# Mixture-of-experts weights fetched with one transfer per matrix instead of four

## The reference, cut to what matters

```python
def ec_moe(x, router_w, w_gate, w_up, w_down):
    bsz, n_tok, _ = x.shape
    cap = n_tok * EC_CAPACITY // N_EXPERTS
    aff = jax.nn.softmax(jnp.einsum('btd,de->bte', x, router_w).astype(jnp.float32), axis=-1)
    gate, idx = lax.top_k(jnp.swapaxes(aff, 1, 2), cap)
    bidx = jnp.arange(bsz)[:, None, None]
    xe = x[bidx, idx]
    hid = jax.nn.silu(jnp.einsum('becd,edf->becf', xe, w_gate)) * jnp.einsum('becd,edf->becf', xe, w_up)
    ye = jnp.einsum('becf,efd->becd', hid, w_down) * gate[..., None].astype(x.dtype)
    return jnp.zeros_like(x).at[bidx, idx].add(ye)
```

## Time and profile before

| | before |
|---|---|
| median of 3 runs | 1393.1 us (1390.18 to 1395.51) |
| the profiled execution, its own time | 1392.07 us |
| its span, first to last instruction | 1390.3 us |
| TensorE busy | 1289.3 us, 93% of the span |
| DVE, ACT, POOL busy | 48%, 35%, 20% |
| bytes moved | 334.27 MB, 240 GB/s on average |
| busy share of the main hardware queue (q1) | 59.0% |
| mean granted TensorE clock | 0.981 |

### The profile page before, as it was taken

How to read it: one execution, slowest core, us unless ns; L and a number is a source line. 1 busy time by engine, 2 the same in 40 slices (tenths; PEclk the granted TensorE clock), 3 DMA queues, 4 the chain that set the end, 5 groups by cost and what they waited for, 6 DMA issues and landing times. The chain is left out here.

```text
span 1390.3 us, 34498 instructions
## 1 busy us (share of the span) xinstructions
PE 1289.3 (93%) x14873; PEld 955.2 (69%) x14873; DVE 665.8 (48%) x1574; ACT 491.9 (35%) x1131; POOL 280.4 (20%) x239
## 2 busy tenths in 40 slices
PE   5999998879899999999989999989999999999996
PEld 1755566756687577777768999555578576777773
DVE  1535614677635243333345646956654433333336
ACT  2723213766423211111125468665533321111113
POOL 0000103596101011111110030645400201111101
PEclk7999999999999999999998999999999999999997
DMA  9688861041448999999982012050065999999985
GB/s 362 233 318 336 334 225 47 5 167 46 157 195 320 365 368 377 375 375 368 369 314 57 1 65 70 1 227 1 1 245 197 391 344 374 376 373 378 376 299 182
DMA packets 105827, 334.27 MB, mean 240 GB/s; under 512 B 23182, under 2 KB 29164, under 8 KB 99532
## 3 DMA queue, kind: packets, MB, share of 16 engines
q1 hardware_dynamic: 99276, 310.11, 59.0%
q0 software_dynamic: 5824, 19.86, 6.1%
q10 hardware_dynamic: 576, 2.10, 0.4%
HBM read 308.13 MB, written 23.89 MB: 239 GB/s over the span
## 5 line engine op out<-in xcount | busy, mean ns | idle before, releaser
L2053 PE MATMUL psum<-proj,wraw 128*64 128x80 f32 x7680 | 285.6, 234 | 14.8 <-issue 14.5
L2053 PEld LDWEIGHTS psum<-proj,wraw 128*64 128x64 f32 x7680 | 272.7, 137 | 32.1 <-issue 29.7
L2102 ACT ACTIVATE proj<-psum,proj 128x64 f32<-128x64 f32 x232 | 67.3, 395 | 289.8 <-PE psum L1981 289.8
L1993 PE MATMUL psum<-wraw,proj 128*32 128x512 f32 x1152 | 156.0, 596 | 2.2 <-ACT proj L2108 1.2
L1959 POOL DMA_INDIRECT x_rows<-modrow,idx x30 | 42.8, 1428 | 430.6 <-DVE modrow L2221 430.6
L2216 DVE SCALAR_TENSOR_TENSOR modrow<-psum,proj 64x512 f32<-64x512 f32 x60 | 44.9, 749 | 132.0 <-PE psum L1999 131.6
L1336 POOL TENSOR_SCALAR ring<-ring,small 128x640 f32<-128x640 f32 x48 | 90.2, 1883 | 40.3 <-DVE small L1275 39.9
L1999 PE MATMUL psum<-wraw,proj 128*16 128x256 f32 x1152 | 96.4, 379 | 1.4 <-issue 0.9
L2176 DVE TENSOR_SCALAR proj<-psum,proj 128x64 f32<-128x64 f32 x232 | 55.7, 317 | 85.4 <-PE psum L1981 85.4
L1999 PEld LDWEIGHTS psum<-wraw,proj 128*16 128x16 f32 x1152 | 35.5, 97 | 80.5 <-issue 73.6
L1266 DVE TENSOR_REDUCE small<-psum 128x1 f32<-128x640 f32 (+1 forms) x80 | 57.3, 716 | 53.8 <-PE psum L1241 53.4
(11 more groups left out here) (524 smaller groups left out, 2366.3 us busy)
## 6 DMA issues: line engine op xcount, KB each, us to landing
wraw<-in_exp_w_gate_dram SPq DMA_DIRECT2D x128, 512.0 KB
wraw<-in_exp_w_up_dram SPq DMA_DIRECT2D x128, 512.0 KB
wraw<-in_exp_w_down_dram SPq DMA_DIRECT2D x128, 512.0 KB
ring<-in_ada_w_dram SPq DMA_DIRECT2D x29, 1024.0 KB, 7.1
hold<-in_ada_w_dram SPq DMA_DIRECT2D x14, 1024.0 KB, 6.7
ring<-in_ev_w_in_dram SPq DMA_DIRECT2D x4, 2048.0 KB, 12.5
xr<-x_rows SPq DMA_DIRECT2D x15, 512.0 KB, 6.6
proj<-in_ada_w_dram SPq DMA_DIRECT2D x5, 1024.0 KB, 8.3
```

Of the source, the lines that this page charges most:

```text
L1993: mm = pe.matmul(psum[quad(q, 32), b, :], xs[:, quad(q % 2, 32)], pair[q // 2], start=first, stop=last)
L2053: mm = pe.matmul(psum[c:c + WT, b, f * CAP:(f + 1) * CAP], wraw[SLOT_OF[m]][:, at:at + WT], rows, start=(k == 0 and f == 0), stop=(k == KD ...
L2102: ins = act.activation(xgT[:, e % 2, k, lo:hi], bank(0)[:, k * CAP + lo:k * CAP + hi], ACT.Identity, scale=scale_of[:, c, k:k + 1], bias=s ...
```

## The change

For all matrices but numbers 4 to 7, `load_weights` issues one transfer of 2 MB where it issued four of 512 KB. In gate and up matrices the row that lands in a partition is now one run of 16 KB. In down matrices it is still four rows of 4 KB. Matrices 4 to 7 still come in four pieces each, as `load_piece` asks for them, and `landed` counts 64 for these and 16 for the others.

```diff
         PARTS = 4
+        IN_PIECES = range(AT_ONCE, AT_ONCE + 4)
...
         def load_weights(sp, l, m, ready):
-            for i in range(PARTS):
-                load_piece(sp, l, m, i, ready)
+
+            n, e = EXPERT_ORDER[m]
+            if n == 2:
+                src, to = A[EXPERT_W[n]][l, e].rearrange("(f p) n -> p f n", p=P), wraw[SLOT_OF[m]][:, :].rearrange("p (f n) -> p f n", f=FB)
+            else:
+                src, to = A[EXPERT_W[n]][l, e].rearrange("(p k) n -> p (k n)", p=P), wraw[SLOT_OF[m]][:, :]
+            sp.dma_start(to, src).then_inc(ready[SLOT_OF[m]], 16)

         def landed(m):

-            return 16 * PARTS * SLOT_OF[:m + 1].count(SLOT_OF[m])
+            return sum(16 * (PARTS if i in IN_PIECES else 1) for i in range(m + 1) if SLOT_OF[i] == SLOT_OF[m])
```

## The result

| | before | after |
|---|---|---|
| median of 4 runs each | 1392.55 us (1390.18 to 1395.51) | 1406.83 us (1402.92 to 1412.28) |
| the profiled execution, its own time | 1392.07 us | 1402.92 us |
| its span | 1390.3 us | 1401.1 us |
| bytes moved | 334.27 MB | 334.25 MB |

The ratio after to before is 1.0104, with a 95% interval of 1.0065 to 1.0143. The forecast was 1393 us, no change. The spans of the two profiled executions are 10.8 us apart.

The account below looks back on a forecast made before the run. The prediction took TensorE plus its instruction-fetch gaps to bound the experts, and DMA the end of layer 0. Terms of -3.9 and +4 us summed to 0 against the 1393.1 us median: 1393 us, range 1381 to 1422.

Parts of the forecast that it names:

- The reading of the bound: While experts run, TensorE plus its gaps is on the path, weights are not; excess over the shortest expert 23.6 us.
- The reading of "issue": Gaps inside TensorE's unbroken products are waits for its next 16 KB of instructions on q8; 5.4 us in 9 gaps.
- Requests on SP, 0: Three of four weight requests fall away on SP, which does nothing else due: worth 0.
- The rate, 426 GB/s: Gate and up rows of 16 KB move at 426 GB/s instead of 399; gains nothing while experts run.
- the rate in 480:700 would rise: Sign in the new profile: during layer 0's experts the rate rises above 373 GB/s.
- The fixed 2 us of a transfer: A fixed 2.0 us per weight transfer, taken from the skill; the prediction held that queued transfers hide it.
- The fetch term, +4: Instruction fetches during experts wait 0.15 us more behind long rows; 8.4 us over 28 experts, half taken: +4 us.
- The end of layer 0, -3.9: At layer 0's end token numbers land before DVE is free, so DVE, ACT and the block's end come 3.9 us earlier.
- The scatter, 0: The experts' scatter lands 2.3 us later behind long rows, covered by 4.0 us of room: 0.
- B: Rival: slower, short instruction and scatter transfers pay for long rows; mostly 1401 to 1420 us, chance 0.36.
- its own sign: Sign of the slower rival by instruction fetches: the mean expert takes over 16.8 us.
- C: Rival: faster, half the weight packets bring fetches sooner and halve TensorE's gaps; 1377 us, chance 0.22.

Follow-up runs that it names:

- e7: Changed kernel, but from matrix 11 on only the first quarter of each matrix is loaded and experts compute with old data; 1366.17 us, one execution.
- e4: Changed kernel with gate and up described as four 4 KB runs in one request, packets still 16384 bytes; 1409.21 us, ratio 1.0102.
- e9: Changed kernel where POOL's two subtractions at the end of layer 0's experts wait for DVE's comparison; 1408.12 us, one execution.
- e1: Changed kernel with down matrices back in four requests, gate and up still one request of 16 KB rows; 1410.08 us, ratio 1.0112.
- e2: Changed kernel with gate and up back in four requests of 4 KB rows, down matrices still in one; 1394.77 us, ratio 1.0006.
- e3b: Changed kernel with gate and up in four requests, each 16 KB rows of every fourth partition, down in four pieces; 1410.01 us, ratio 1.0124.
- e11: Kernel before the change, with the token numbers asked for by ACT instead of SP; 1392.99 us, ratio 0.9983.
- e4b: Changed kernel with gate and up in two requests of alternate 4 KB runs, packets 4096 bytes, down in one request; 1398.59 us, ratio 1.0030.

## Why the prediction was wrong

**The reading of the bound held.** No wait of TensorE for weights appears while experts run, before or after, and its excess of 23.6 us goes with the DMA load (e7: 15.50 us for each expert). The reading of "issue" as the fetch of instructions was right as well: 21.0 of 23.6 us before and 29.4 of 32.5 after stand at every 256th instruction, behind the end of a q8 packet.

**Requests on SP, 0:** held; no wait of TensorE for a transfer appeared. **The rate, 426 GB/s:** 429 measured for rows of 16 KB alone, and 0 within the stretch: held. Only the sign was wrong that the rate in 480:700 would rise; it fell to 365, since TensorE asked for weights more slowly. The fixed 2 us of a transfer, which the prediction takes from the Trainium skill (DMA: Bandwidth & Descriptors, section Anatomy of one DMA), is given there for transfers that GpSimd asks for; no run here measures it for SP's.

**The fetch term, +4, is one step that failed, by its size.** The mechanism was there, "A packet of q8 or q0 that comes up while one is under way waits half of it on average", priced at 0.15 us. Measured, a fetch ends 0.20 us later on average in the changed kernel's trace, and 0.28 and 0.35 us later in e4 and e9, whose expert code is the same. Then came "two of the 2.6 fetches of an expert show": 32 of 62 showed before and 37 after, 1.3 and 1.5 of 2.6 per expert. Last, half of the product was taken, for a lower bound ("an engine may take turns within a row") that nothing supported. The term was +4 us; the experts grew by 11.7 us in the profiled pair. Even the full 8.4 us would have been too little. Why a fetch comes later by more than half a long row stays open. That rows of 16 KB cause the delay is shown by e1, e2 and e3b and by the table of places; how many rows a fetch waits for, no run counts.

**The end of layer 0, -3.9, is the other step that failed.** The token numbers did come earlier, though 0.65 us behind DVE and not ahead of it. The step that broke is "So DVE starts 722.05 - 718.13 = 3.9 us earlier ... and ACT and the block's end follow." The comparison met POOL's subtractions and took 4.51 us instead of 1.51, 3.0 of the 3.9 us; the distance from filler to block went from 12.63 to 12.38. That POOL stood there was in the trace of before (721.27), and the 1.51 us of the earlier trace rows against 0.55 in layer 1 was the sign. e9 and e11 show that 3.4 to 3.9 us are there when the two don't meet.

**The scatter, 0:** held. It lands 2.2 us later (2.3 had been worked out for it), 11.7 at most, and DVE's L2222 still waited for TensorE alone. The gather, which had no term, lands 4.4 us later (13.6 against 9.2, medians in 465:700), and TensorE's waits name it nowhere.

**The rivals.** B came true at its low end, 1406.8 in "1401 and 1420", by the fetches and not by the scatter; by its own sign, a mean expert over 16.8 in one layer and just under in the other. The stated range, 1381 to 1422, holds the result by the share that B had in it, not by the terms of the forecast. C's premise was right (the gaps exist only where the engines are loaded), its conclusion not: half the packets didn't bring fetches sooner. The rule of the Trainium skill on taking turns packet by packet (DMA: Bandwidth & Descriptors, section Queues, rings and completion order) stood beside B. Its packet is a group of descriptors and not the single row that the profile calls one, and e3b against e2 agrees with it only so far as that longer rows cost the small queue more.

**Open** is why e4b costs 0.3%, why rows of 2 KB bring fetches later and not sooner (4.82 against 4.64 us), why a fetch loses more than half a long row, and whether long rows really help when the engines aren't full.

## What to carry to other kernels

Where TensorE runs long unrolled code while the DMA engines are full, its instruction fetches can come too late, and the rows of the bulk transfers bear on the price: from 4 to 16 KB each fetch came 0.20 to 0.35 us later on average (0.25 with as many requests as before), which made 1% of the time here, though the long rows alone move 7.5% faster. With rows of 4 and 8 KB the number of requests may have a part too, at most 0.3%. The gaps can be told in a trace: "issue" inside unbroken runs of products, every 256 instructions, just behind a q8 packet. Before counting an earlier arrival as a gain, look at what the freed engine will then run beside: DVE against POOL above all. And a mechanism with a worked-out price shouldn't be halved because its lower bound is zero, least of all when half a row is itself only the mean of the plainest case.

## What was unexpected in the hardware

DVE's comparison of 80x640 took 0.55 us alone and 4.51 us (5.24 in e7) beside two POOL subtractions of 4.32 us together.

A transfer to 32 neighbouring partitions ran each 16 KB packet in 1.17 us instead of 0.62, with every fourth partition at full speed. Runs that a transfer describes apart but that lie side by side are joined into one packet.

TensorE's clock after the wait at layer 0's end. Before, with 5.67 us idle ahead of them, the next block's products of 80x512 took 0.63 us and the granted clock of 732:745 was 0.59. In e9, with 1.52 us idle, the first six behind the opening one took 0.39 or 0.40 us, at the level of 2.4 GHz, and from 740.05 on 0.63, as at 1.2; the granted clock was 1.00 in 729:738 and 0.74 in 738:751. The block's first 100 products took 20.95 us there, against 21.82 in the changed kernel. The idle time alone doesn't decide it: in e2 3.51 us of it went before first products of 0.39 us, in e11 2.26 us before ones of 0.63 us from the start.
